# Layer 0 of a two-layer diffusion trunk: another order of first loads, first modulation columns and first low halves

## The reference

```
def trunk_layer(x, cond, lp_norm, lp_mix, lp_moe, ctx, lam_init):
    norm_mix_l, norm_ffn_l, w_mod_l, b_mod_l = lp_norm
    mod = jax.nn.silu(cond) @ w_mod_l + b_mod_l
    sh1, sc1, g1, sh2, sc2, g2 = jnp.split(mod[..., None, :], 6, axis=-1)
    h = rmsnorm(x, norm_mix_l) * (1.0 + sc1) + sh1
    y, new = mixer_sublayer(h, lp_mix, ctx, lam_init)
    x = x + g1 * y
    ...
```

## Time and profile before

| | us |
|---|---|
| median of 3 runs | 1683.08 |
| lowest and highest | 1682.74, 1683.67 |
| profiled execution: span | 1681.4 |
| median less span | 1.7 |
| PE busy in the span | 1653.9 (98%) |
| DVE, ACT, POOL busy | 996.6, 862.5, 644.5 |
| first matmul of GEMM unit 0 begins | 29.03 |
| first matmul of GEMM unit 4 begins | 53.33 |

### The profile page before, as it was taken

How to read it: one execution, slowest core, us unless ns; L and a number is a source line. 1 busy time by engine, 2 the same in 40 slices (tenths; PEclk the granted TensorE clock), 3 DMA queues, 4 the chain that set the end, 5 groups by cost and what they waited for, 6 DMA issues and landing times.

```text
span 1681.4 us, 26841 instructions
## 1 busy us (share of the span) xinstructions
PE 1653.9 (98%) x10047; PEld 1340.6 (80%) x10047; DVE 996.6 (59%) x1662; ACT 862.5 (51%) x1455; POOL 644.5 (38%) x408
## 2 busy tenths in 40 slices
PE   8999999999999999999999999999999999999998
PEld 7788887777888887777778888777778888877776
DVE  3136567563451179999850384775634413899997
ACT  2443344545443347888644334454545334488884
POOL 0644464334467711000135554534345665100102
PEclk9999999999999999999999999999999999999999
DMA  9723344354557669999865334344354665699994
GB/s 354 266 88 110 107 151 126 107 181 139 188 205 247 206 222 403 382 380 377 306 233 196 97 112 139 114 130 139 132 192 153 223 216 176 249 400 376 380 370 162
DMA packets 128112, 367.23 MB, mean 218 GB/s; under 512 B 12028, under 2 KB 42364, under 8 KB 128000
## 3 DMA queue, kind: packets, MB, share of 16 engines
q1 hardware_dynamic: 93872, 319.80, 52.6%
q10 hardware_dynamic: 27504, 21.74, 4.2%
q0 software_dynamic: 6624, 24.18, 3.9%
HBM read 341.71 MB, written 23.97 MB: 217 GB/s over the span
## 4 chain that ended last, share of the span: by engine, by line
PE 83%; DVE 7%; DMA 3%; issue 3%; ACT 2%; POOL 1%; SPq 1%; POOLq 0%; ACTq 0%; DVEq 0%
PE G L1392 20%; PE G L1394 18%; PE G L1393 18%; PE S L1392 3%; PE S L1394 3%; PE S L1393 3%; DVE pA L1931 2%; PE T L1718 2%; PE O L1468 2%; DVE wlo L1931 2%; PE O L1749 2%; PE S L1704 2%; DMA x_scratch<-pA 2%; DVE prob L1931 1%; PE T L1622 1%
## 5 line engine op out<-in xcount | busy, mean ns | idle before, releaser
L857 POOL TENSOR_TENSOR wlo<-raw,whi 128x1024 fp32r<-128x1024 f32 x198 | 489.2, 2476 | 556.4 <-ACT whi L1006 556.3
L1392 PE MATMUL G<-whi,hhi 128*128 128x512 f32 (+1 forms) x1440 | 578.3, 402 | 9.5 <-DVE wlo L1931 5.6
L1394 PE MATMUL G<-whi,hlo 128*128 128x512 f32 (+1 forms) x1440 | 558.4, 388 | 0.0
L1393 PE MATMUL G<-wlo,hhi 128*128 128x512 f32 (+1 forms) x1440 | 557.8, 387 | 0.0
L1392 PEld LDWEIGHTS G<-whi,hhi 128*128 128x128 f32 x1440 | 270.8, 188 | 84.3 <-DVE wlo L1931 14.9
L1394 PEld LDWEIGHTS G<-whi,hlo 128*128 128x128 f32 x1440 | 270.7, 188 | 57.3
L1393 PEld LDWEIGHTS G<-wlo,hhi 128*128 128x128 f32 x1440 | 271.4, 188 | 46.5
L1006 ACT ACTIVATE whi<-raw 128x1024 fp32r<-128x1024 f32 x204 | 214.7, 1054 | 100.1 <-PE G L1394 67.7
L1931 DVE TENSOR_TENSOR wlo<-raw,whi 128x1024 fp32r<-128x1024 f32 x150 | 181.7, 1225 | 13.8 <-ACT whi L1014 9.7
L1014 ACT ACTIVATE whi<-raw 128x1024 fp32r<-128x1024 f32 x144 | 152.4, 1060 | 29.2 <-PE G L1394 16.5
L1931 DVE TENSOR_TENSOR wlo<-pA,whi 128x1024 fp32r<-128x1024 f32 x72 | 88.0, 1225 | 29.4 <-ACT whi L1014 25.9
(11 more groups left out here) (405 smaller groups left out, 2302.6 us busy)
## 6 DMA issues: line engine op xcount, KB each, us to landing
raw<-in_units SPq DMA_DIRECT2D x423, 512.0 KB, 5.2
pA<-in_units SPq DMA_DIRECT2D x78, 512.0 KB, 5.7
pB<-in_units SPq DMA_DIRECT2D x72, 512.0 KB, 6.0
h_sorted<-sig POOLq DMA_DIRECT2D x12, 514.0 KB, 7.3
hs<-h_sorted POOLq DMA_DIRECT2D x10, 514.0 KB, 7.3
y_sorted<-yo POOLq DMA_DIRECT2D x10, 512.0 KB, 7.0
bias<-in_nat_bias ACTq DMA_DIRECT2D x16, 256.0 KB, 3.7
pB<-rows_scratch ACTq DMA_DIRECT2D x8, 512.0 KB, 9.4
```

The lines of the kernel that those rows point to most:

```text
L857: lo_done.of(nc.gpsimd.tensor_tensor(wlo[:, k, :], raw[:, POS_OF[g] % RAW, :], whi[:, k, :].bitcast(F32), ALU.subtract))
L1392: nc.tensor.matmul(dst, st_hi, mv_hi, start=start, stop=False)
L1393: nc.tensor.matmul(dst, st_hi, mv_lo, start=False, stop=False)
L1394: return nc.tensor.matmul(dst, st_lo, mv_hi, start=False, stop=stop)
```

## The change

What it does, part by part:
- SP loads the tokens first, then quad 0, `pcol`, unit 0, quad 1, GEMM unit 1 (position 5), then positions 1 to 4.
- Four constant tables (`tri`, `cmask`, `rope`, `order`) are loaded by SP behind `small`, and no longer by ACT.
- Ahead of GEMM unit 0 only quad 0 is made, with column blocks 0 and 1. Quad 1 with blocks 2 and 3 is made inside unit 0, quad 2 inside unit 1, quad 3 inside unit 2, each time behind token tile 0.
- POOL makes the low halves of units 0, 1 and 2, which DVE made before.
- Layer 0 neither saves the tokens nor waits for that; `loadX` reads them from the input.
- Layer 1 keeps its order (`SCHEDULES[1]`).

```diff
@@ schedule
+    quad2 = [("mod", j) for j in range(NEXT, NEXT + MQ)]
+    if first:
+        put_inside(0, 1, ("quad1",))
+        put_inside(1, 1, *quad2)
+        put_inside(2, 1, ("quad3",))
+    else:
+        put(0, *quad2)
+        put(1, ("quad3",))
@@ sync
-            for q in range(NEXT // MQ):
+            def first_quad(q):
                 for j in range(MQ * q, MQ * q + MQ):
                     next_mod(first_home[j], j, 0).then_inc(nx_in[q].handle, 16)
...
+            for t in range(TILES):
+                sp.dma_start(x[:, t, :], a["tokens"][t]).then_inc(tokens_in, 16)
+            first_quad(0)
...
+                if l == 0:
+                    load(0)
+                    first_quad(1)
+                    load(POS_OF[1])
+                    for p in range(1, POS_OF[1]):
+                        load(p)
...
+                if l == 0:
+                    for dst, src in ((tri[:, :, :], a["tri"]), (cmask[:, :, :], a["cmask"]), (rope_t[:, :, :], a["rope"]),
+                                     (order[:, :], a["order"])):
+                        sp.dma_start(dst, src).then_inc(const_in, 16)
...
-                    elif s == ("dma", "saveX"):
-                        sp.wait_ge(tokens_in, 16 * TILES)
+                    elif s == ("dma", "saveX") and l > 0:
@@ gpsimd
+                        for g in range(CONV) if l == 0 and s[1] == 0 else ():
+                            split(g)
@@ scalar
                         xn_act.of(nc.scalar.activation(xn[:, 1, :], x[:, 1, :], ACT.Copy, scale=st[:, 1:2]))
+                        if l == 0:
+                            split(0)
                         for c in range(KD):
                             act.wait_ge(*hf_dve.at(l, c))
                             hh_act.of(nc.scalar.activation(hhi[:, c, :], chunk(c), ACT.Copy))
+                            if l == 0:
+                                if c == 1:
+                                    split(1)
+                                elif c == 3:
+                                    split(2)
+                                    late_rows(0)
+                                elif c == 5:
+                                    split(3)
+                                    late_rows(1)
+                                continue
...
-                                    if arg == "Aq" and t == 0:
+                                    if arg == "Aq" and t == 0 and l > 0:
                                         act.wait_ge(*x_saved.at(l, 0))
...
-                        x_in.of(act.dma_start(x, a["x_scratch"].rearrange("t p n -> p t n")))
+                        x_in.of(act.dma_start(x, a["tokens" if l == 0 else "x_scratch"].rearrange("t p n -> p t n")))
@@ tensor
+            for _ in range(BUSY_FIRST):
+                nc.tensor.matmul(S[:, 0, 0:P], ident[:, :], ident[:, :], start=True, stop=True)
+            pe.wait_ge(nx_in[0].handle, 16 * MQ)
+            first_quad(0)
...
+                    elif s == ("quad1",):
+                        columns(2)
+                        columns(3)
+                        pe.wait_ge(nx_in[1].handle, 16 * MQ)
+                        pe.wait_ge(nx_dve.handle, 1)
+                        first_quad(1)
+                        pe.wait_ge(nx_act.handle, 2)
+                        first_turned(1)
+                        read["O"] = (nx_dve, -1)
@@ vector
                         for c in range(KD):
+                            if l == 0 and c in (0, 2):
+                                first_rows(c // 2)
+                                first_cols(c // 2)
...
-                            if c == 1:
+                            if l == 0:
+                                if c % 2:
+                                    low(c - 1)
+                                    low(c)
+                            elif c == 1:
```

More of the change, by code:

```diff
@@ L110, with schedule @@
 assert DEPTH == 2
-def schedule():
+def schedule(first):
     after = {g: [] for g in range(-1, NG)}
@@ L229, in mod_block, with tiles_of @@
     return KD * g + 2 * q + i
-SCHEDULE = schedule()
-def tiles_of(s):
-    cuts = [0] + [r[2] for r in SCHEDULE if r[0] == "rest" and r[1] == s[1]] + [TILES]
+SCHEDULE = schedule(False)
+SCHEDULES = (schedule(True), SCHEDULE)
+def tiles_of(l, s):
+    cuts = [0] + [r[2] for r in SCHEDULES[l] if r[0] == "rest" and r[1] == s[1]] + [TILES]
     n = cuts.index(s[2]) if s[0] == "rest" else 0
@@ L728, in _ @@
                 pc_in.of(sp.dma_start(pcol[:, :], layer_of("pcol").rearrange("a p n -> p (a n)")))
-                for p in range(RAW):
-                    released(p - RAW)
-                    load(p)
+                if l == 0:
[4 more added lines that the diff above has]
+                        load(p)
+                else:
+                    for p in range(RAW):
+                        released(p - RAW)
+                        load(p)
                 sp.wait_ge(*layer_end.at(l, -1))
@@ L868, in _ @@
                 first = True
-                for s in SCHEDULE:
+                for s in SCHEDULES[l]:
                     if s[0] == "norm":
@@ L1360, in next_turned, with first_quad, first_turned @@
                 return mm
[L1362 to L1365, removed]
-                next_quad(q, first_home, lambda mm: mm.then_inc(nx_pe.handle, 1))
-            pe.wait_ge(nx_act.handle, 1)
-            next_turned().then_inc(nxt_pe.handle, 1)
-            pe.wait_ge(nx_dve.handle, 1)
+            def first_quad(q):
+                for k in range(KD):
+                    for i in range(MQ):
+                        mm = nc.tensor.matmul(O[32 * i:32 * i + 32, 2 * q * P:(2 * q + 1) * P], cond[:, k, :],
+                                              first_home[MQ * q + i][:, k * P:(k + 1) * P], start=(k == 0), stop=(k == KD - 1))
+                        if k == KD - 1:
+                            mm.then_inc(nx_pe.handle, 1)
+            def first_turned(q):
+                nc.tensor.transpose(O[:, (2 * q + 1) * P:(2 * q + 2) * P], mrow[:, q * P:(q + 1) * P],
+                                    ident[:, :]).then_inc(nxt_pe.handle, 1)
+            for _ in range(BUSY_FIRST):
+                nc.tensor.matmul(S[:, 0, 0:P], ident[:, :], ident[:, :], start=True, stop=True)
+            pe.wait_ge(nx_in[0].handle, 16 * MQ)
+            first_quad(0)
             for l in range(layers):
@@ L1373, in need @@
                 def need(s, i):
-                    if i > passed.get(s.name, -1):
+                    if i > passed.get(s.name, -2):
                         passed[s.name] = i
```

65 lines of the change are left out of this document (37 added, 28 removed).

## The result

The changed kernel took 1686.84 us in the median of 20 runs (1683.83 to 1690.66), the kernel before 1683.36 in the same comparison (1680.00 to 1688.38, 20 runs). The ratio is 1.0019, with a 95% interval of 1.0011 to 1.0026: 1.9 to 4.4 us slower. By the prediction's bound of 0.2% that is no change, though the interval lies wholly above 1. The predicted step was +1.9 us, the predicted time 1685.0.

A forecast was written before the change was run, and what follows sets the result against it. PE was taken to bound the kernel, busy 1653.9 of 1681.4 us. Unit 4's later low half (+0.7) and PE's slow restart (+1.2) gave +1.9 on 1683.1, so 1685.0, range 1681.0 to 1687.4.

The forecast's parts named there:

- bound of 0.2%: On the whole time: 3.4 us, about what a measurement of this kernel can tell from no change.
- its likeliest case: Whole time within 0.2% of the kernel before, chance 0.78; faster and slower had 0.11 each.
- The same bytes at the same rate: Loads ahead of unit 2: reordered but the same set, so it lands at 36.7 again, a zero term.
- The copy waits for unit 2's landing, and PE waits for the copy: Inside unit 1: quad 2's row copy stands behind unit 2's high half on ACT; turn at 38.25, PE stands some 6 us.
- The stall for the saved tokens is gone, but unit 4's low half is what is late next: Ahead of unit 4: the 2.01 us stall goes, the low half sets the start at 54.0 against 53.33, +0.7.
- The restart: PE after its wait inside unit 1: slow first matmuls lose 1.5 us, 0.33 of it covered, leaving +1.2.
- the rival's 2.48 for all twelve: Unit 1 after PE's wait: all twelve matmuls run slow, 2.48 us longer, 1686.0; chance 0.11.
- The estimate that the prediction made from the Trainium skill: Unit 1 after PE's wait: all twelve matmuls at the lower clock level would lose 2.5 us, giving 1686.3.
- GpSimd's low half of unit 2 is ready at 40.2, so it hides: Ahead of unit 2, beginning at 41.43: the low half is ready with 1.2 us to spare.
- the step behind quad 3's turn: From quad 3's turn to the end of unit 4's low half: 8.54 us as before, all work unchanged.
- What unit 4 moves by is what the end moves by: Behind unit 4's beginning both kernels run the same work, so its shift is the shift of the end.

The follow-up runs named there:

- C: The changed kernel, but SP issues unit 2 behind quad 2's units, ahead of quad 3, `prow`, `small` and the tables; ratio 0.9985 to the kernel before.
- I: The changed kernel with the four tables back on ACT's queue, behind the tokens; ratio 1.0018 to the kernel before.
- B: The changed kernel with ACT making unit 2's high half behind quad 2's row copy and blocks 4 and 5, ahead of unit 3's; ratio 1.0026.
- G: The kernel before, without saving the tokens, waiting for the save or loading the copy in layer 0; ratio 0.9991.
- H: The changed kernel with layer 0's saving of the tokens, its wait and the load from the saved copy put back; ratio 1.0012.
- E: The changed kernel with unit 2's low half made by DVE, not GpSimd; ratio 1.0023 to the kernel before.
- F: The changed kernel with sixteen filling matmuls ahead of PE's wait for quad 2's rows and unit 2's low half made by DVE; ratio 1.0023.
- J: The changed kernel with unit 2 loaded early, as in C, and 28 instead of 12 early filling matmuls; ratio 0.9982 to the kernel before.
- K: J with quad 3's row copy ahead of unit 3's high half on ACT as well; ratio 0.9988 to the kernel before.
- D: The changed kernel with sixteen short filling matmuls ahead of PE's wait for quad 2's row copy; ratio 1.0017 to the kernel before.

## Why the prediction was right, and where its sum was off

It was right in its likeliest case: a change within 0.2%, on the slower side, by the wait that it named. Step by step:

| step | predicted | measured |
|---|---|---|
| unit 2 is taken up | 36.7 | 37.05 |
| unit 0 begins | 19 to 22.2 | 22.04 |
| PE in front of quad 2's turn | 32 to 35 | 34.26 (38.32 - 4.06) |
| quad 2's turn | 38.25 | 38.32 |
| lost in the twelve matmuls | 1.5 | 2.30 |
| low half of block 4 | 41.43 | 43.0 |
| unit 2 begins | 42.6 | 43.60 |
| quad 3's turn, from there | 4.01 | 4.07 |
| from that turn to unit 4's low half | 8.54 | 8.16 |
| unit 4, less before | +1.9 | +2.58 |

**"The same bytes at the same rate"** held to 0.35 us. C shows that the bytes ahead were the reason, and I that their queue was not.

**"The copy waits for unit 2's landing, and PE waits for the copy"** held. B adds what the prediction did not say: without that queue position PE would wait for the low half of unit 2 instead, almost as long.

**"The stall for the saved tokens is gone, but unit 4's low half is what is late next"** held: the chain ends on it, and G and H give the stall's worth in either order, 1.8 and 0.

**The restart** was mis-sized for this execution. I took 1.5 us from the slow first burst; 2.30 were lost, close to the rival's 2.48 for all twelve, and this with 0.2 more at the turn is the whole way of unit 2 from 42.6 to 43.60. The estimate that the prediction made from the Trainium skill (TensorE: Matmul & The Clock Gate, Part 1), 2.5 us, is nearer as well, and the granted clock of 0.55 bears it out. (Its 1686.3 leaves out the 0.33 us of cover that the rival's 1686.0 counts.) But behind nearly the same rest E, H and I lost 1.59, 1.38 and 1.58, so 1.5 was a fair size, and the loss differs between executions.

**"GpSimd's low half of unit 2 is ready at 40.2, so it hides"** is the step that failed. It hides from PE, which needs it at 43.60, but not from DVE: the gain step is held for 1.28 us, and so block 4's low half is 1.6 late. In H and I, where fewer matmuls were slow, this alone puts unit 2 at 43.26 and 43.13; in the changed kernel's execution the slow matmuls cover it. I looked for who waits for GpSimd's result, not for who works beside it. The trace before had the sign: DVE's two low halves, 1.24 us at 38.53, took 1.59 beside POOL's low half of unit 3.

```profile
43.73 2.40 POOL L857 TENSOR_TENSOR wlo<-raw,whi 128x1024 fp32r<-128x1024 f32 x1 [23.12 <-ACT whi L1006]
...
45.43 1.59 DVE L1931 TENSOR_TENSOR hlo<-probT,hhi 128x384 fp32r<-128x384 f32 x2
```

At unit 4 the two together are 1.33, by F, where the sum had 1.2 for the restart alone; the step behind quad 3's turn gave 0.38 back, which is luck.

**"What unit 4 moves by is what the end moves by"** does not hold for single executions. The profiled ones differ by 1.8 us more behind unit 4, and 1.75 of that is the clock near 610 us (5.15 against 3.40 us lost). As B lost 1.70 there and H 3.45, I do not put it down to the change. The digit 9 in every slice of the earlier trace rows hid the loss of the kernel before, since it stands for 0.9 and more.

## What to carry to other kernels

When a product is made to start earlier, follow its later operands to their place in the load queue: the order of bytes decides, not the time of the issue, and moving a consumer in its own queue only moves the wait. A long wait of PE can be paid twice, in the wait and in the slow matmuls behind it. Of two delays that lie side by side, removing one shows little. Before work goes to GpSimd because its result is not urgent, look at which DVE instructions run beside it and who waits for those.

## What the runs showed of the hardware

- A DVE instruction with SBUF inputs that meets a running GpSimd instruction is held to its end: `acol` 1.45 us instead of 0.17, its second step 2.40 instead of 0.16, two low halves 5.03 instead of 1.23. The one that reads PSUM, `modc`, is not held (0.17).
- PE's waits of 4.06, 4.17, 3.95, 3.75 and 3.60 us (changed kernel, E, I, H, B) were followed by eleven, about eight, eight, seven and six matmuls some 0.43 us apart, in B with slow passes of quad 3 behind them. In E, I and H the first one to five matmuls still ran at the full clock. The waits of 2.29 and 3.15 us ahead of unit 0 (J, K) were followed by slow matmuls too; 1.69 us at that place (C) and 2.01 us in the kernel before were not. With sixteen short matmuls in the wait (D, F), none was slow.
- Near 610 us, in layer 0's routing, the clock falls to the lower level in every profiled execution, at places and for times that vary. PE is busy throughout there. Here are the changed kernel and the kernel before by windows; what starts it stays open.

```profile
605.00:610.00 5.00, 5.00 (x57) 4.67 (x55) 2.33 (x9) 1.90 (x4) 1.10 (x2) 0.66 0.40 119
610.00:615.00 5.00, 5.00 (x85) 4.48 (x81) 4.76 (x18) 0.00 (x0) 0.00 (x0) 0.50 0.00 0
615.00:620.00 5.00, 5.00 (x60) 4.55 (x51) 2.64 (x11) 0.77 (x2) 0.00 (x0) 0.81 0.92 332
...
605.00:610.00 5.00, 5.00 (x84) 4.38 (x80) 4.69 (x20) 0.00 (x0) 0.00 (x0) 0.50 0.02 3
610.00:615.00 5.00, 5.00 (x80) 4.68 (x73) 3.96 (x16) 0.38 (x1) 0.00 (x0) 0.83 0.66 218
```
